# Triangular inverses of a four-mixer layer: 32x32 blocks on four array tiles, and 64x64 products that cross the partition halves

## The reference, cut to what matters

```python
a_kk = einsum('bnhid,bnhjd->bnhij', kb, k) * exp(where(strict, seg, -inf))
sol = lax.linalg.triangular_solve(a_kk, rhs, left_side=True, lower=True, unit_diagonal=True)
w, u = sol[..., :dk], sol[..., dk:]
def step(s, xs):
    v_new = u_n - w_n @ s
    o_n = q_n @ s + aqk_n @ v_new
    s = s * g_last + k_n.T @ v_new
```

## Time and profile before

| | |
|---|---|
| median of 3 runs | 2915.53 us |
| the profiled execution, first to last instruction | 2922.9 us |
| scan in `deltanet` | 737 to about 1017 us of the span |
| scan in `rwkv` | 1198 to about 1523 us |
| PE, DVE, ACT, POOL busy over the span | 89%, 53%, 34%, 29% |
| inverse products (L1348 and L1356), PE busy | 277.4 + 47.2 us |
| their wait before them | 69.7 + 10.1 us |

### The profile page before, as it was taken

One profiled execution on the slowest core, in us unless ns is written; L12 is line 12 of the kernel. 1 busy time (PEld: TensorE's weight loads), 2 busy tenths in 40 slices (PEclk: granted clock), 3 DMA queues, 4 the chain that ended last, 5 costly groups with the idle time before them and its releaser, 6 DMA issues. The chain is left out here.

```text
span 2922.9 us, 78835 instructions
## 1 busy us (share of the span) xinstructions
PE 2601.6 (89%) x30395; PEld 1471.9 (50%) x30396; DVE 1537.2 (53%) x2779; ACT 985.8 (34%) x1687; POOL 835.3 (29%) x654
## 2 busy tenths in 40 slices
PE   5999899799789779788888987989999999999956
PEld 2448358455788745588874434333333333333322
DVE  3106375654366522444443466666666666666628
ACT  2603116212222113222211111445555555555511
POOL 1000000000333100111100000556666666666655
PEclk9999998899999889999998999999999999999988
DMA  6001302300000020000013213889898989782277
GB/s 248 1 13 38 127 15 87 105 15 1 3 4 4 3 70 0 2 4 4 4 43 112 87 55 125 325 336 349 350 367 316 355 327 344 269 315 92 79 288 309
DMA packets 109125, 408.53 MB, mean 140 GB/s; under 512 B 21001, under 2 KB 37083, under 8 KB 83932
## 3 DMA queue, kind: packets, MB, share of 16 engines
q1 hardware_dynamic: 76636, 287.71, 26.6%
q0 software_dynamic: 20736, 75.51, 6.7%
q10 hardware_dynamic: 11520, 41.95, 3.6%
HBM read 346.40 MB, written 58.72 MB: 139 GB/s over the span
## 5 line engine op out<-in xcount | busy, mean ns | idle before, releaser
L3287 PE MATMUL bank<-arena 128*32 x1280 | 568.7, 597 | 9.6 <-SPq L68 6.7
L3289 PE MATMUL bank<-arena 128*32 128x512 f32 x3840 | 569.8, 597 | 0.0
L3248 POOL COPY arena<-arena 128x2048 f32 x240 | 448.8, 1904 | 329.3 <-PE bank L3321 312.3
L1348 PE MATMUL bank<-arena 64*64 64x64 f32 x8320 | 277.4, 219 | 69.7 <-DVE arena L1444 19.7
L3287 PEld LDWEIGHTS bank<-arena 128*32 128x32 f32 x1280 | 134.9, 110 | 358.5 <-issue 349.5
L1348 PEld LDWEIGHTS bank<-arena 64*64 64x64 f32 x8320 | 260.1, 135 | 81.5 <-DVE arena L1444 22.4
L3318 PE MATMUL bank<-arena 128*32 x640 | 289.2, 595 | 5.5 <-POOL arena L3248 5.5
L3321 PE MATMUL bank<-arena 128*32 128x512 f32 x1920 | 290.3, 595 | 0.0
L3442 DVE COPY arena<-arena 128x2048 f32 x80 | 138.4, 1731 | 200.5 <-PE bank L3289 183.6
L3379 ACT COPY arena<-arena 128x2048 f32 x80 | 152.0, 1900 | 200.1 <-PE bank L3289 143.5
L3238 POOL DMA_INDIRECT arena<-normed_rows,arena x80 | 166.1, 2076 | 149.6 <-DVE arena L3426 137.8
(11 more groups left out here) (561 smaller groups left out, 4550.0 us busy)
## 6 DMA issues: line engine op xcount, KB each, us to landing
arena<-in_exp_w_gate_dram SPq DMA_DIRECT2D x64, 1024.0 KB, 6.1
arena<-in_exp_w_up_dram SPq DMA_DIRECT2D x64, 1024.0 KB, 8.8
arena<-in_exp_w_down_dram SPq DMA_DIRECT2D x64, 1024.0 KB, 9.5
expert_rows<-arena ACTq DMA_DIRECT2D x80, 512.0 KB, 8.2
arena<-in_w_mod_dram SPq DMA_DIRECT2D x32, 512.0 KB, 7.7
arena<-in_x_dram SPq DMA_DIRECT2D x16, 512.0 KB, 6.6
arena<-in_w_mod_dram SPq DMA_DIRECT2D x8, 1024.0 KB, 18.4
arena<-in_w_in_dram SPq DMA_DIRECT2D x12, 384.0 KB, 5.3
```

The lines of the kernel that those rows point to most:

```text
L1348: last = self.nc.tensor.matmul(self.banks[bank][r, x * HD:(x + 1) * HD], lhsT[r, x], rhs[r, x], start=True, stop=True)
L3248: last = nc.gpsimd.tensor_copy(down_copy(u), down_of(slots[u]))
L3287: nc.tensor.matmul(out(SUB - 1), XTT[:, b.q, c, rows(SUB - 1)], W[:, :, c], start=first, stop=end)
L3289: last = nc.tensor.matmul(out(u), XTT[:, b.q, c, rows(u)], WC[:, u, :, c], start=first, stop=end)
```

## The change

`Solve` keeps the diagonal 32x32 blocks alone: partitions are taken in four quarters (`quad(g)`, 32 partitions each), and M, N, X, T and the new C are buffers of 8x32 = 256 columns. A product (`blocks`, L1275 of the new kernel) is 32 matmuls of 32x32, 8 blocks in 4 quarters, on four 32x32 tiles of the array. C takes Y's place through stage 6. Stage 7 multiplies the off-diagonal 32x32 block of N64 with C, and its result goes to the neighbouring quarter. Stage 8 writes the whole 64x64 blocks of Y: X times the unit matrix for the diagonal blocks, which turns X back, and X times T for the others, 64 matmuls. Copies and adds of ACT and DVE in stages 0 to 7 are 128x256 in place of 128x512; in stage 8 DVE copies 128x512 where it added 128x512. Waits and semaphores stay as they were, and so do the masks on POOL.

In `rwkv` one of the two products in each of `gram_k`, `gram_q` and `gram_t` now writes to the other partition half (`across`), and the two products are issued in turn, two matmuls of one and two of the other, so that neighbouring matmuls stand on all four 64x64 tiles. The half that N, AB and TB lie in has changed by that, so `right`'s product into `b_u` and `result`'s products cross too. The class `Inverse` is deleted; nothing used it.

```diff
+def across(n):
+    return half(1 - n)
+def quad(g):
+    return slice(QD * g, QD * g + QD)
+def own(g):
+    return slice(QD * (g % 2), QD * (g % 2) + QD)
...
-        self.M, self.N, self.X, self.T = (cr.take(8, HD) for _ in range(4))
+        self.M, self.N, self.X, self.T, self.C = (cr.take(8, QD) for _ in range(5))
...
-    def product(self, bank, lhsT, rhs):
+    def blocks(self, bank, lhsT, rhs):
         for x in range(8):
-            for a in range(2):
-                r = half(a)
-                last = self.nc.tensor.matmul(self.banks[bank][r, x * HD:(x + 1) * HD], lhsT[r, x], rhs[r, x],
+            for g in range(4):
+                r = quad(g)
+                last = self.nc.tensor.matmul(self.banks[bank][r, x * QD:(x + 1) * QD], lhsT(r, g, x), rhs(r, g, x),
                                              start=True, stop=True)
...
         elif k == 7:
             self.dve_done(pe, p, 6)
-            last = self.product(1, N64, Y)
+            for x in range(8):
+                for g in range(4):
+                    to = quad(g ^ 1)
+                    last = self.nc.tensor.matmul(self.banks[1][to, x * QD:(x + 1) * QD], N64[quad(g), x, other(g)],
+                                                 self.C[quad(g), x], start=True, stop=True)
         else:
             self.act_done(pe, p, 7)
-            last = self.product(2, self.X, self.T)
+            for x in range(8):
+                for col, rhs in ((own, unit), (other, T)):
+                    for g in range(4):
+                        r, at = quad(g), x * HD + col(g).start
+                        last = self.nc.tensor.matmul(self.banks[2][r, at:at + QD], self.X[r, x], rhs(r, g, x), start=True,
+                                                     stop=True)
...
+        elif k == 8:
+            last = self.nc.vector.tensor_copy(self.Y[:, p % 2], self.banks[2].rearrange("p (x j) -> p x j", x=8))
...
-            def gram(bank, lhsT, rhs):
+            def grams(crossed, straight):
                 for x in range(8):
-                    for a in range(2):
-                        r = half(a)
-                        last = nc.tensor.matmul(bank[r, x * HD:(x + 1) * HD], lhsT[r, x], rhs[r, x], start=True,
-                                                stop=True)
+                    for bank, (lhsT, rhs), to in ((b_b, straight, half), (b_a, crossed, across)):
+                        for a in range(2):
+                            r = half(a)
+                            last = nc.tensor.matmul(bank[to(a), x * HD:(x + 1) * HD], lhsT[r, x], rhs(r, x), start=True,
+                                                    stop=True)
...
-                            last = nc.tensor.matmul(b_s[r, at:at + HD], TB[r, p % 2, x], UU[r, d * 2 + q],
+                            last = nc.tensor.matmul(b_s[across(a), at:at + HD], TB[r, p % 2, x], UU[r, d * 2 + q],
                                                     start=False, stop=(at == 3 * HD))
```

More of the change, by code:

```diff
@@ L1191, in _ @@
                     nc.vector.tensor_tensor(g, g, k.ps[1 + 2 * n + h][:, :], ALU.add)
[L1194 to L1290, removed]
@@ L1293, in half, with other @@
+QD = HD // 2
 def half(n):
     return slice(HD * n, HD * n + HD)
+def across(n):
[4 more added lines that the diff above has]
+    return slice(QD * (g % 2), QD * (g % 2) + QD)
+def other(g):
+    return slice(QD * (1 - g % 2), QD * (1 - g % 2) + QD)
 def chunk(step, d):
@@ L1319, in build @@
             nc.vector.tensor_copy(self.l64[r], k.lvl[64][r, r])
-            last = nc.vector.tensor_copy(self.ident[r], k.ident[r, r])
+            nc.vector.tensor_copy(self.ident[r], k.ident[r, r])
+            for g in (2 * a, 2 * a + 1):
+                last = nc.vector.tensor_copy(self.unit[quad(g)], k.ident[quad(g), quad(g)])
             chain(last)
@@ L1342, in dve_done @@
         eng.wait_ge(self.dve_s, p * self.NDVE + self.DVE_AT[k] + 1)
-    def product(self, bank, lhsT, rhs):
+    def blocks(self, bank, lhsT, rhs):
         for x in range(8):
-            for a in range(2):
-                r = half(a)
-                last = self.nc.tensor.matmul(self.banks[bank][r, x * HD:(x + 1) * HD], lhsT[r, x], rhs[r, x],
[L1349 to L1353, removed]
-            for a in range(2):
-                r = half(a)
-                last = self.nc.tensor.matmul(self.banks[bank][r, x * HD:(x + 1) * HD], src[r, x], self.c.ident[r],
+            for g in range(4):
+                r = quad(g)
+                last = self.nc.tensor.matmul(self.banks[bank][r, x * QD:(x + 1) * QD], lhsT(r, g, x), rhs(r, g, x),
                                              start=True, stop=True)
@@ L1374, in tensor @@
                 self.dve_done(pe, p - 1, 8)
-            self.product(0, self.M, self.N)
-            self.product(1, self.N, self.M)
-            last = self.product(2, self.N, Y)
+            self.blocks(0, M, N)
+            self.blocks(1, N, M)
+            last = self.blocks(2, N, C)
         elif k == 3:
@@ L1385, in tensor @@
             self.dve_done(pe, p, 3)
-            last = self.product(2, self.N, Y)
+            last = self.blocks(2, N, C)
         elif k == 5:
             self.dve_done(pe, p, 4)
-            self.turn(0, Y)
-            last = self.product(1, N32, Y)
+            self.blocks(0, C, unit)
+            last = self.blocks(1, level(N32), C)
         elif k == 6:
@@ L1426, in vector @@
         dve.wait_ge(self.pe_s, p * self.NPE + k + 1)
-        b = [bank[:, :].rearrange("p (x j) -> p x j", x=8) for bank in self.banks]
-        TT, Y = self.nc.vector.tensor_tensor, self.Y[:, p % 2]
+        b = [bank[:, 0:8 * QD].rearrange("p (x j) -> p x j", x=8) for bank in self.banks]
+        TT, C = self.nc.vector.tensor_tensor, self.C
         if k == 0:
             self.act_done(dve, p, 0)
-            last = TT(Y, self.M, each(self.c.ident, 8), ALU.add)
+            last = TT(C, self.M, each(self.c.unit, 8), ALU.add)
         elif k == 1:
@@ L2378, in gram_k @@
                     pe.wait_ge(tb, p)
-                gram(b_a, ZS[:, p % 3], BS)
-                gram(b_b, KS, ZS[:, p % 3]).then_inc(n_ps, 1)
+                z = lambda r, x: ZS[r, p % 3, x]
+                grams((ZS[:, p % 3], lambda r, x: BS[r, x]), (KS, z)).then_inc(n_ps, 1)
             def gram_q(p):
@@ L2385, in gram_q @@
                 pe.wait_ge(azk, p + 1)
-                gram(b_a, BS, RS[:, p % 3])
-                gram(b_b, KS, RS[:, p % 3]).then_inc(q_ps, 1)
+                q = lambda r, x: RS[r, p % 3, x]
+                grams((BS, q), (KS, q)).then_inc(q_ps, 1)
             def gram_t(p):
@@ L2392, in gram_t @@
                     pe.wait_ge(abr, p - FIRST + 1)
-                for src, bank in ((BS, b_a), (KS, b_b)):
-                    for x in range(8):
-                        for a in range(2):
-                            r = half(a)
-                            last = nc.tensor.matmul(bank[r, x * HD:(x + 1) * HD], src[r, x], H.ident[r], start=True,
-                                                    stop=True)
-                last.then_inc(t_ps, 1)
+                unit = lambda r, x: H.ident[r]
+                grams((BS, unit), (KS, unit)).then_inc(t_ps, 1)
             def right(p, u):
```

39 lines of the change are left out of this document (20 added, 19 removed).

## The result

| | before | changed |
|---|---|---|
| median of the runs on one chip | 2918.2 us | 3153.4 us |
| lowest to highest, 4 runs each | 2914.6 to 2921.1 | 3147.9 to 3158.6 |
| the profiled execution, first to last instruction | 2922.9 us | 3152.7 us |
| mean granted clock of that execution | 0.957 | 0.884 |

The changed kernel is slower: ratio 1.0806, 95% interval 1.0788 to 1.0823, 235 us. The forecast was 2810 us and its range ended at 2960.

The account below looks back on a forecast made before the run. Scans bound by PE's record rate, then the chain of stages. Pairs fall 3.8 us in `deltanet` and 7.4 in `rwkv`, ten each: -112 us, +6 for the clock, so 2915.5 - 106 = 2810 us; range 2780 to 2960.

Parts of the forecast that it names:

- What bounds the kernel now: Both scans: bound by PE's rate of records, 29.2 ns each, then by the chain of stages.
- What a 32x32 record costs: Inverse on PE: 31.5 ns per tile, 7.9 ns a record on four tiles, so 1,024 records take 8.1 us a pair.
- The bound above: Slowest 32x32 record expected: 29.2 ns, the fastest rate over runs beyond 32 records, should feeding instructions set it.
- Rival C: TensorE's instruction fetch: 85 packets more; with 2 us unhidden latency each, 24 ns a record, time as at 25; chance 0.04.
- Rival B: PE's issue binds hard: 29.2 ns for every 32x32 record, +277 us, 3193 us; chance 0.07.
- Packets: TensorE's instruction queue: 85 packets more than the 178 before, about 263.
- Changes of shape: PE switching between 32x32 and 64x64: 0.16 us each, +1.9 us a pair in `deltanet`, +1.8 in `rwkv`.
- Copies and adds: Inverse: ACT's fall from 586 to 380 ns, DVE's from 688 to 421, costing only where PE waits.
- Crossing: `rwkv` grams: 192 records on four tiles at 14.6 ns, 2.8 for 5.6 us a pair; rival of no overlap: chance 0.08.
- Clock: Scans: +6 us for a lower granted clock; as a rival, falling for a fifth of PE work, +70 us; chance 0.07.

Follow-up runs that it names:

- experiment 1: All phases left out, TensorE alone multiplying constant tiles, written out or looped: 2,048 32x32 records took 55.2 us written out, 1,792 took 18.2 us in the loop.
- experiment 3: The changed kernel with the 64x64 inverse of the kernel before, so only the crossing is left: 2900.1 us, ratio 0.9935 to the kernel before.
- experiment 4: The changed kernel without the crossing, only the inverse packed to 32x32 blocks: 3146.7 us, ratio 1.0772 to the kernel before.

## Why the prediction was wrong

- **What bounds the kernel now.** Right: products at 29.2 ns a record on two tiles are bound by the tiles; in the loop, where nothing is fetched, they take the same 30.08 us for 1,024 as written out. Overlooked: a packet of them is 128 x 29.3 = 3.75 us, and the supply needs about 3.5. The kernel before ran just above a floor that the profile did not name, and 29.2 ns, read as the speed of the tiles, was nearly that of the supply too.
- **What a 32x32 record costs: the step that failed.** As the prediction put it: 7.9 ns, "since one, two and four tiles all give the same time per tile". As time of the tiles it was right: 8.3 ns inside a packet on four tiles, 32 on one. But the price that a pair pays is 27 ns or more, 3.5 to 3.75 us a packet, so 1,024 records cost some 28 to 30 us and not 8.1. The bound above was set right, at 29.2 ns, and then given too little weight, because the only faster row was a run of 32 records: a quarter of one packet, too short to meet a packet's edge. The earlier trace rows are from a loop, `experts`, where nothing is fetched: in the kernel before, the queue of the earlier trace rows brings no packet between 1900 and 2700 us.
- **Rival C had the mechanism**, with 0.04 of the chances. It took 1.05 us for a packet and guessed 2 us of latency unhidden, 24 ns a record and 3107 us. It was held off by "a packet's worth goes in 2.0 us, so it keeps up", and that is a slip: a packet is 256 instructions, 128 records, and at 7.9 ns they go in 1.0 us, less than even the transfer takes. One packet is fetched while another runs, as C supposed, but it comes 3.45 us after the start of the one before at best, since 1.04 us pass before its transfer and 1.47 us behind it (experiment 1). At the 3.45 to 3.75 us that TensorE alone shows, its 10.25 and 11.5 packets a pair are 35.4 to 38.4 and 39.7 to 43.1 us, against 38.4 and 43.8 measured; what is left are packets of up to 4.0 us and waits that had no room in them, which I have not told apart. Rival B came near in time (3193, pairs of 41.2 and 43.9) and had feeding as the limit as well, but as a rate for each record, and it added the waits and changes of shape, most of which the pauses cover.
- **Packets.** 263 forecast and found. The count was there; its price was not. The kernel before could not show it by their distance, 126 us / 30 = 4.2 us, which is the pace of its own products.
- **Changes of shape.** 0.16 us forecast, 0.15 measured in the loop; under the pauses they don't show.
- **Copies and adds.** ACT's are 0.37 us and DVE's 421 ns as forecast. They save nothing, since both engines wait for PE.
- **Crossing.** The step was right: 14.4 ns a record for 14.6, 2.3 us a pair for 2.8. It only pays in a kernel that isn't bound by the supply (experiment 3), so in the changed one it is lost (experiment 4).
- **Clock.** It fell further than forecast, to 0.71 and 0.72 in the scans, where PE now stands idle at the packets' edges; in experiment 1 it was 0.50 in the same case, but also while one tile alone kept PE busy without a pause, so idleness is not all that lowers it. It lengthens 128 records of 32x32 from 1.27 to 1.93 us, which still ends before the next packet is there, so in such packets it is a consequence and costs nothing. 64x64 products suffer more: a gram of 64 records that starts at 1396.41 in the changed kernel takes 1.99 us, against 1.1 in experiment 3. What the clock costs in packets filled with such products was not measured by itself.

## What to carry to other kernels

Count TensorE's instructions in straight-line code (a float32 matmul is four) and set 3.5 us per 256 of them beside the work that these do; the larger of the two counts, packet by packet, since only one is fetched ahead. Making products smaller and more numerous pays only while their packets still hold more than 3.5 us of work, or in a loop whose body stays under some 1,500 instructions. A rate read from a run shorter than 128 records, or from a loop, says nothing of a long written-out run. What shares tiles better without a further instruction, as the crossing, is worth doing, and by itself gave 0.65%.

## What the runs showed that I had not expected

- TensorE's supply: a packet of 256 instructions every 3.45 us at best, often 3.7 to 4.0, in a row of about 1.0 us from the start of one packet to the transfer of the next, 0.9 to 1.1 of transfer and 1.4 from its landing to the first record; 4.4 us of pause at a jump back to code that is no longer held. 1,536 instructions stay, 2,048 do not.
- 32x32 products at the full clock: 8.3 ns a record on four tiles, 32 on one tile alone (53 at the lower level). A jump back in a loop costs 0.30 us.
- 64x64 products on four tiles: 14.4 ns a record in a gram and 15.9 in a loop, 29.3 on two.
- Open: why packets come 3.45 us apart at one time and 3.7 to 4.0 at another.
